# Tokens beside the last output tile, late products on TensorE, and row sums as columns, in a two-layer transformer kernel

## The reference

```python
for l in range(2):
    sh, sc, g = split(silu(c) @ w_mod[l] + b_mod[l])      # the same with c_ctx for the context tokens
    h = x * (1 + sc) + sh                                  # modulated tokens
    q, k, v, z = split(h @ w_in[l])
    y = neighbourhood_attention(q, k, v) if l == 0 else differential_attention(q, k, v)
    out = (y * silu(z)) @ w_out[l]
    x = layer_norm(ALPHA * x + (1 + g) * out)              # layer 0: the context tokens too
```

## Time and profile before

| | |
|---|---|
| median of 3 runs | 1866.39 us (1865.43 to 1867.48) |
| the profiled execution | 1866.36 us, its span 1864.3 us |
| TensorE busy | 1807.0 us, 97% of the span |
| VectorE busy | 1303.2 us, 70% |
| ScalarE busy | 928.0 us, 50% |
| GpSimd busy | 270.6 us, 15% |
| mean granted TensorE clock | 0.994 |

### The profile page before, as it was taken

How to read it: one execution, slowest core, us unless ns; L and a number is a source line. 1 busy time by engine, 2 the same in 40 slices (tenths; PEclk the granted TensorE clock), 3 DMA queues, 4 the chain that set the end, 5 groups by cost and what they waited for, 6 DMA issues and landing times. The chain is left out here.

```text
span 1864.3 us, 30823 instructions
## 1 busy us (share of the span) xinstructions
PE 1807.0 (97%) x10617; PEld 1557.2 (84%) x10617; DVE 1303.2 (70%) x2061; ACT 928.0 (50%) x1680; POOL 270.6 (15%) x219
## 2 busy tenths in 40 slices
PE   7999999999999999989989999999999999999997
PEld 3888888888988888868868988888888888898886
DVE  6677777777777868775867576674848484757658
ACT  2555555555555555550045545464737464554500
POOL 3100000000000000256331010101001010102951
PEclk9999999999999999989999999999999999999999
DMA  9512121213121212225411010101010000101343
GB/s 346 133 48 81 50 82 46 82 47 84 45 80 43 79 54 62 89 76 185 157 68 35 12 45 11 39 6 45 11 34 23 34 23 11 45 11 45 98 153 113
DMA packets 81967, 127.28 MB, mean 68 GB/s; under 512 B 49744, under 2 KB 49904, under 8 KB 81792
## 3 DMA queue, kind: packets, MB, share of 16 engines
q1 hardware_dynamic: 76048, 108.54, 18.8%
q0 software_dynamic: 2384, 8.39, 1.6%
q10 hardware_dynamic: 3488, 9.73, 1.3%
HBM read 108.90 MB, written 20.09 MB: 69 GB/s over the span
## 5 line engine op out<-in xcount | busy, mean ns | idle before, releaser
L536 PE MATMUL acc<-h_hi,w_hi 128*128 128x512 f32 (+1 forms) x1408 | 524.7, 373 | 2.4 <-DVE h_lo L461 1.3
L536 PE MATMUL acc<-h_hi,w_lo 128*128 128x512 f32 (+1 forms) x1408 | 509.1, 362 | 0.0
L536 PE MATMUL acc<-h_lo,w_hi 128*128 128x512 f32 (+1 forms) x1408 | 508.3, 361 | 0.0
L536 PEld LDWEIGHTS acc<-h_hi,w_lo 128*128 128x128 f32 x1408 | 265.5, 189 | 41.5
L536 PEld LDWEIGHTS acc<-h_hi,w_hi 128*128 128x128 f32 x1408 | 266.0, 189 | 38.7 <-DVE h_lo L461 3.7
L536 PEld LDWEIGHTS acc<-h_lo,w_hi 128*128 128x128 f32 x1408 | 266.4, 189 | 34.0
L1645 DVE TENSOR_REDUCE stats<-acc 128x1 f32<-128x1280 f32 x128 | 189.7, 1487 | 43.3 <-PE acc L1739 42.7
L1562 ACT ACTIVATE far_prob<-acc,stats 128x1280 f32<-128x1280 f32 x128 | 170.2, 1330 | 28.3 <-DVE stats L1645 26.5
L1569 ACT ACTIVATE far_pt<-acc 128x512 f32<-128x512 f32 (+1 forms) x192 | 101.1, 527 | 162.1 <-PE acc L1748 158.6
L1739 PE MATMUL acc<-k_dup,q_stack 128*128 128x512 f32 (+1 forms) x768 | 176.8, 367 | 1.8 <-ACT far_prob L1562 0.4
L1761 PE MATMUL acc<-far_pt,far_v 128*128 128x128 f32 x1280 | 172.7, 275 | 0.0
(11 more groups left out here) (192 smaller groups left out, 2920.5 us busy)
## 6 DMA issues: line engine op xcount, KB each, us to landing
w_raw<-in_w_in SPq DMA_DIRECT2D x64, 512.0 KB, 3.4
near_late_slots<-in_w_mod SPq DMA_DIRECT2D x64, 256.0 KB, 2.6
w_raw<-in_w_out SPq DMA_DIRECT2D x16, 512.0 KB, 3.3
w_raw<-y_t POOLq DMA_DIRECT2D x14, 448.0 KB, 5.2
y_t<-y SPq DMA_DIRECT2D x7, 640.0 KB, 3.0
modulation_rows<-in_w_scale SPq DMA_DIRECT2D x8, 512.0 KB, 6.9
modulation_rows<-in_w_mod SPq DMA_DIRECT2D x8, 512.0 KB, 6.7
out_rows<-in_x SPq DMA_DIRECT2D x8, 512.0 KB, 4.6
```

The lines of the kernel that those rows point to most:

```text
L536: mm = nc.tensor.matmul(m.bank(self.bank_of(j, c), w), wt[:, b % 2, k, :], ht[:, k, t0:t0 + w], start=(k == 0 and i == 0), stop=(k == KT - ...
```

## The change

It has three parts.

**Tokens beside the last output tile.** Tile 9's output product is cut into its eight k. After each, TensorE does `turn(0, k)`, and `mm_done` counts each k. `take_hi(0, k)` waits for the k-th piece alone, since that piece is the last reader of `h_hi[:, k]`. VectorE mixes tile 8's layer norm with `take_lo` of group 0, and tile 9's with that of group 1. ScalarE's `root` and `store` of these tiles move between its modulations, and so does the split of projection weights 1. For group 2, products follow turns at a distance of four.

**The last chunk.** Tile 5 is summed in step 3, and tiles 6 and 7 not on VectorE at all: `reduce_last` multiplies their 128x128 blocks with the two condition columns on TensorE and adds them to the accumulators' sums in PSUM. The load of tile 7 moves up between the loads of output weights 3 and 4. The output weights' high parts are taken one step earlier from the second on (two in step 2). The fillings move: two pieces in each of the steps 5, 7 and 9 in place of one in each of 4 to 9; the one at the end of step 9 stays.

**Row sums as columns.** In every chunk the accumulators' 128x128 blocks become the weights and a column of ones the moving operand, so the sums land as eight columns (4 blocks x 2 conditions) on 128 partitions. ScalarE copies 128x8, and SP stores them with two transfers of single 4-byte elements. The buffer is no longer shared with `factors`, so one wait of ScalarE goes (`repeat_factors`).

The diff, without the hunks for `ones` in place of `pick`, the name `cols` and the end count 32 in place of 16:

```diff
--- before.py
+++ after.py
...
@@ -167,8 +167,8 @@
         self.late_acc = sb("late_acc", [P, 2, 512])
-        self.shared = sb("row_or_factors", [P, 512])
-        self.late_row, self.factors = self.shared[0:2, :], self.shared[:, 0:2 * P]
+        self.shared = sb("cols_and_factors", [P, 2 * P + 8])
+        self.factors, self.late_cols = self.shared[:, 0:2 * P], self.shared[:, 2 * P:2 * P + 8]
...
@@ -399,22 +397,42 @@
+    def sums(self, bank, t, first, count):
+        return self.m.psum[:, bank, 2 * t + first:2 * t + first + count]
...
         pe.wait_ge(self.summed, CREDIT + c * 2 * KT + 2 * KT)
-        for cnd in range(2):
-            mm = self.nc.tensor.matmul(self.m.psum[0:2, bank, :], self.m.pick[:, cnd, :], self.acc[cnd],
-                                       start=(cnd == 0), stop=(cnd == 1))
+        for t in range(4):
+            for cnd in range(2):
+                mm = self.nc.tensor.matmul(self.sums(bank, t, cnd, 1), self.acc[cnd][:, t * P:(t + 1) * P], self.m.ones[:, :],
+                                           start=True, stop=True)
...
+    def reduce_last(self, pe, c, bank):
+        for u in (KT - 2, KT - 1):
+            pe.wait_ge(self.loaded[u % 2], CREDIT + c * 8 * KT + 16 * (u // 2 + 1))
+        pe.wait_ge(self.summed, CREDIT + c * 2 * KT + 2 * (KT - 2))
+        for t in range(4):
+            for u in (KT - 2, KT - 1):
+                self.nc.tensor.matmul(self.sums(bank, t, 0, 2), self.slots[u % 2][:, t * P:(t + 1) * P], self.m.cond_act[:, :, u],
+                                      start=(u == KT - 2), stop=False)
+            for cnd in range(2):
+                mm = self.nc.tensor.matmul(self.sums(bank, t, cnd, 1), self.acc[cnd][:, t * P:(t + 1) * P], self.m.ones[:, :],
+                                           start=False, stop=(cnd == 1))
+        mm.then_inc(self.reduced, 1)
     def take_row(self, act, c, bank):
-        act.wait_ge(self.row_stored, CREDIT + c * 16)
+        act.wait_ge(self.row_stored, CREDIT + c * 32)
         act.wait_ge(self.reduced, CREDIT + c * 1 + 1)
-        self.nc.scalar.activation(self.row, self.m.psum[0:2, bank, :], ACT.Copy, scale=0.5).then_inc(self.row_ready, 1)
+        self.nc.scalar.activation(self.cols, self.m.psum[:, bank, 0:8], ACT.Copy, scale=0.5).then_inc(self.row_ready, 1)
...
         sp.wait_ge(self.row_ready, CREDIT + c * 1 + 1)
-        sp.dma_start(self.mod_rows[:, bass.ds(c * 512 + ROW_PAD, 512)], self.row).then_inc(self.row_stored, 16)
+        for cnd in range(2):
+            dst = self.mod_rows[cnd, bass.ds(c * 512 + ROW_PAD, 512)].rearrange("(t p) -> p t", p=P)
+            sp.dma_start(dst, self.cols.rearrange("p (t c) -> p c t", c=2)[:, cnd, :], allow_slow_non_contiguous=True).then_inc(self.row_stored, 16)
@@ -1005,8 +1023,8 @@
     filled = {step: piece[0:2] for (step, half), piece in fill.items() if piece[3] == KT}
-    fill_last = {(4, MIDDLE): (0, 1), (5, MIDDLE): (1, 2), (6, MIDDLE): (2, 3), (7, MIDDLE): (3, 4), (8, MIDDLE): (4, 5),
-                 (9, MIDDLE): (5, 6), (9, END): (6, 7)}
+    fill_last = {(5, MIDDLE): (0, 2), (7, MIDDLE): (2, 4), (9, MIDDLE): (4, 6), (9, END): (6, 7)}
+    OUT_SPLITS = {2: (0, 1), 3: (2,), 4: (3,), 5: (4,), 6: (5,), 7: (6,), 8: (7,)}
@@ -1072,6 +1090,8 @@
                             out_w.load(sp, p, k)
+                            if k == 3:
+                                late.load(sp, c, 7)
@@ -1081,9 +1101,8 @@
                             load_bias(biases[1], c, kind)
-                    late.load(sp, c, 7)
                     if not last:
-                        for u in (KT, KT + 1):
+                        for u in (7, KT, KT + 1):
...
@@ -1178,8 +1197,6 @@
                         act.wait_ge(recip_done, CREDIT + c * COLS + (col + 1))
-                        if col == 0:
-                            act.wait_ge(late.row_stored, CREDIT + c * 16)
@@ -1211,8 +1228,9 @@
                             p.split_hi_part(act, c, 5)
-                        if 2 <= step < 2 + KT and last:
-                            out_w.split_hi(act, p, step - 2)
+                        if last:
+                            for k in OUT_SPLITS.get(step, ()):
+                                out_w.split_hi(act, p, k)
@@ -1299,7 +1317,9 @@
                             p.split_lo_part(v, nc.vector, c, 5)
-                        if NU - 3 <= step < NU:
+                        if step == 3 and last:
+                            late.sum(v, c, 5)
+                        if NU - 3 <= step < NU and not last:
@@ -1426,7 +1446,10 @@
                                 pe.wait_ge(p.evac, CREDIT + (c + 1) * p.evacs + 3)
-                            late.reduce(pe, c, 1 if last else 7)
+                            if last:
+                                late.reduce_last(pe, c, 1)
+                            else:
+                                late.reduce(pe, c, 7)
@@ -1502,9 +1525,10 @@
                 p.split_lo_part(pool, nc.gpsimd, 0, 0)
-                pool.wait_ge(before.mm_done, TOK_TILES)
...
                     for k in range(KT):
+                        if g == 0:
+                            pool.wait_ge(before.mm_done, TOK_TILES + k)
@@ -1537,15 +1561,19 @@
                 p.split_hi_part(act, 0, 0)
-                before.act_tile(act, TOK_TILES - 2)
...
                     tokens.modulate(act, 0, k)
-                before.root(act, TOK_TILES - 1)
-                act.wait_ge(before.mm_done, TOK_TILES)
-                p.split_hi_part(act, 0, 1)
+                    if k == 1:
+                        before.root(act, TOK_TILES - 2)
+                    if k == 5:
+                        before.store(act, TOK_TILES - 2)
...
                     tokens.modulate(act, 1, k)
+                    if k == 5:
+                        act.wait_ge(before.mm_done, before.done(TOK_TILES - 1))
+                        p.split_hi_part(act, 0, 1)
+                before.root(act, TOK_TILES - 1)
@@ -1617,24 +1645,31 @@
                 before.dve_start(v)
-                for i in range(TOK_TILES - 1):
+                for i in range(TOK_TILES - 2):
                     before.dve_tile(v, i)
-                v.wait_ge(before.mm_done, TOK_TILES)
+                last = TOK_TILES - 2
+                before.take_product(v, last)
+                before.add_residual(v, last)
...
                     tokens.take_lo(v, 0, k)
-                    if k == 1:
-                        before.take_product(v, TOK_TILES - 1)
-                    if k == 4:
-                        before.add_residual(v, TOK_TILES - 1)
-                before.moments(v, TOK_TILES - 1)
+                    if k == 0:
+                        before.moments(v, last)
+                    if k == 2:
+                        before.centre(v, last)
+                    if k == 3:
+                        before.normalise(v, last)
+                last = TOK_TILES - 1
+                before.take_product(v, last)
+                for k in range(KT):
+                    tokens.take_lo(v, 1, k)
+                    if k == 0:
+                        before.add_residual(v, last)
+                    if k == 3:
+                        before.moments(v, last)
...
                 p.split_lo_part(v, nc.vector, 0, 1)
-                for k in range(KT):
-                    tokens.take_lo(v, 1, k)
-                    if k == 1:
-                        before.centre(v, TOK_TILES - 1)
-                    if k == 3:
-                        before.normalise(v, TOK_TILES - 1)
+                before.centre(v, last)
+                before.normalise(v, last)
@@ -1703,15 +1738,19 @@
             def _(pe):
-                before.pe_part(pe)
-                pe.wait_ge(before.normed, 4)
-                pe.wait_ge(before.psum_free, TOK_TILES - 1)
-                for k in range(KT):
+                def turn_first(k):
+                    if k == 0:
+                        pe.wait_ge(before.normed, 4)
+                        pe.wait_ge(before.psum_free, TOK_TILES - 2)
                     tokens.turn(pe, 0, k)
+                before.pe_part(pe, turn_first)
...
                     pe.wait_ge(tokens.lo_done, k + 1)
+                    if k == 0:
+                        pe.wait_ge(before.psum_free, TOK_TILES - 1)
@@ -1719,11 +1758,12 @@
                 pe.wait_ge(before.normed, TOK_TILES)
-                for k in range(KT):
-                    tokens.turn(pe, 2, k)
-                for k in range(KT):
-                    pe.wait_ge(tokens.lo_done, 2 * KT + k + 1)
-                    p.product_part(pe, 0, 2, k, k + 1)
+                for n in range(KT + BEHIND):
+                    if n < KT:
+                        tokens.turn(pe, 2, n)
+                    if n >= BEHIND:
+                        pe.wait_ge(tokens.lo_done, 2 * KT + n - BEHIND + 1)
+                        p.product_part(pe, 0, 2, n - BEHIND, n - BEHIND + 1)
@@ -1976,7 +2016,7 @@
         gain, first = self.gain[i // LAT_TILES], self.bank_of(i, 0)
```

(22 more changed lines are left out.)

## The result

The changed kernel takes 1874.9 us (median of 6 runs, 1872.8 to 1879.5) against 1866.4 before (6 runs, 1865.4 to 1867.5). The ratio is 1.0047, with a 95% interval of 1.0036 to 1.0057. The forecast was 1852.3 us, with a range of 1848.5 to 1859.5. The profiled execution of after is the slowest of its six (1879.5 us, span 1877.7), so its losses are some 4 us above the median's.

A forecast was written before the change was run, and what follows sets the result against it. The prediction took TensorE, busy 97% of the span, as the bound, so gains come from filling its holes or shortening its list. 1866.4 - 8.2 - 5.5 - 0.4 = 1852.3 us, range 1848.5 to 1859.5.

The forecast's parts named there:

- The stores: Row-sum stores in every chunk: 1024 single-element pieces take 4.7 us over 16 engines, hidden, so counted as nothing.
- waits in ordinary chunks behind SP's stores: Sign that the forecast is wrong: TensorE waiting in ordinary chunks behind the row-sum stores; no size given.
- the rival with the stores: End of layer 0: element stores delay the barrier, 58.8 us late if on one engine, total 1911; chance 0.03.
- Part A: Tokens beside tile 9: interleaving turns with its product recovers TensorE's waits and half clock; gain 8.2 us, ends 6.4 and 9.9.
- The 1.7 us that I gave back: Tokens, before product (0,3): a new TensorE wait behind VectorE and the split of weights 1, taken off 9.9 us.
- The ring of three: Tokens: three buffers become the bound as GpSimd and VectorE slow each other; gain only 3 us, 1857.5; chance 0.12.
- group 2 gained nothing: Tokens, group 2: 6.7 us set by the ScalarE, GpSimd and VectorE chain, which interleaving doesn't shorten; gain counted as nothing.
- Part B: Last chunk of layer 0: removing VectorE's sums from steps 7 to 9 gains 5.5 us net, ends 3 and 7.
- where I had said about 15: Last chunk, sign of being right: steps 8 to 10 take about 15 us.
- where I had said under 1: Last chunk, sign of being right: TensorE's waits for `y` in step 9 fall under 1 us.
- where I had 3.4: Last chunk, `reduce_last`: sixteen small float32 products, 32 instructions, take 3.4 us in place of 1.8.
- Part C: Row sums as columns in seven chunks: 0.1 us less each, gain taken as 0.4 us, ends -1.0 and +0.8.

The follow-up runs named there:

- 1024 elements 64 bytes apart: Kernel with tokens' and last chunk's parts and row stores, plus 1024 extra 4-byte element stores per ordinary chunk, each 64 bytes from the next: 1853.0 us.
- the two extra places side by side: Kernel with tokens' and last chunk's parts and row stores, plus 1024 extra packed elements per ordinary chunk, the second 2 KB right behind the first: 1853.0 us.
- both parts and row stores: Changed kernel keeping the tokens' and last chunk's parts, but with the sums back as two rows stored in contiguous 2 KB pieces: 1853.2 us.
- the rows side by side: Changed kernel with its element stores, but a chunk's two rows adjacent in HBM instead of 16.9 KB apart, readers following: 1853.6 us.
- 16-byte pieces: Changed kernel with column sums stored as 128 pieces of 16 bytes per condition instead of 512 single elements: 1855.5 us.

## Why the prediction was wrong, step by step

**The stores were the step that failed.** I worked out 4.7 us for 1024 pieces from the queue's mean time of a packet and placed them under "the next use of those queues is tens of us away". Both halves were wrong. The mean was over other packets: the element writes have hardly any time of their own in the records (9 ns each), but packed sixteen to each 64 bytes, in two places far apart, they hold up what comes behind them, so `y`'s store lands in 20.1 us. And the next use is not tens of us away: it is 2.2 us away (`y`), 3.6 for the next weights, and the engines themselves turned out to depend on the block's end: ScalarE and VectorE stopped some 10 us behind the stores, TensorE 17. I had put it at nothing; the cost is 1874.9 - 1853.6 = 21.3 us. I had listed "waits in ordinary chunks behind SP's stores" as a sign of being wrong, but given it no price; the rival with the stores was put at the block's end, where only a little happened. There, after's wait in front of layer 1's first product is 1.45 us; with the tokens alone it is 0.33:

```profile
868.99 0.69 PE L2077 MATMUL acc<-h_hi,k_dup 128*128 128x512 f32 x2 [1.45 <-PEq L1072]
...
847.16 0.70 PE L2054 MATMUL acc<-h_hi,k_dup 128*128 128x512 f32 x2 [0.33 <-PEq L1054]
```

The Trainium skill, DMA: Bandwidth & Descriptors, Rules for kernel authors, warned of a last dimension that isn't contiguous. Its advice would have saved this kernel, but its reason, one descriptor for each element, isn't what cost the time here: 1024 elements 64 bytes apart cost nothing measurable.

**Part A was right in its size, with one loss in another place.** Forecast 8.2 us, measured 7.9. From the start of layer 1's block to the end of group 2, the trace of the kernel with the tokens alone has 966.62 - 847.16 = 119.5 us, before 975.85 - 848.25 = 127.6. Turns and products alternate, the clock stays at 1 (window, columns as above), and of the waits for modulated tokens 1.0 us is left:

```profile
925.00:967.00 42.00, 40.86 (x224) 32.77 (x223) 32.00 (x43) 18.51 (x31) 20.24 (x25) 1.00 0.21 76
...
PE acc L536 <- DVE h_lo L461: 0.8, 2, 0.5
PE acc L536 <- DVE w_lo L519: 0.2, 1, 0.2
```

The 1.7 us that I gave back came too, but elsewhere, so that the sum fits so closely is in part luck. From 938.02 to group 2 at 959.94 are 21.9 us, against 19.9 of work. The 2.0 lost are small holes within product (0,1), whose pieces follow `take_lo` at up to 1.1 us in place of 0.69:

```profile
951.42 0.50 PE L536 MATMUL acc<-h_hi,w_hi 128*128 128x512 f32 x1
952.23 0.40 PE L536 MATMUL acc<-h_hi,w_hi 128*128 128x512 f32 x1
953.23 0.50 PE L536 MATMUL acc<-h_hi,w_hi 128*128 128x512 f32 x1
954.36 0.50 PE L536 MATMUL acc<-h_hi,w_hi 128*128 128x512 f32 x1 [0.17 <-DVE w_lo L519]
```

The ring of three was not the bound, and group 2 gained nothing, as forecast.

**Part B was right.** Forecast 5.5 us. In after, the last chunk from its predecessor's row sums (754.36) to the products behind its steps (848.87) takes 94.5 us, before 830.66 - 730.59 = 100.1: a gain of 5.6. With row sums it is 95.3, a gain of 4.8, and 4.8 by the medians. That execution has the granted clock at 0.5 for 3.4 us from 792.8 on; the kernel with the two extra places side by side, with row sums too, has none there and takes 94.4. TensorE's waits from 730 to 850 with both parts and row stores, beside the earlier trace rows, show that 7.0 and 2.5 us became 3.5 and nothing. 1.5 us are new, 1.3 of them behind the sum of tile 5, and those for `near_pt_lo` in front of the factors' transposes grew from 2.3 to 3.5:

```profile
PE acc L1399 <- DVE y L1282: 3.5, 4, 1.6
PE acc L1384 <- DVE near_pt_lo L1274: 3.5, 4, 0.9
PE acc L1375 <- DVE near_pt_lo L1274: 1.5, 2, 1.3
```

From step 7's value products (810.92) to the products behind the steps (826.15) it takes 15.2 us there, where I had said about 15. The wait for `y` in step 9 is 1.2 us, where I had said under 1. `reduce_last` takes 847.97 - 844.48 = 3.5 us in after, where I had 3.4.

**Part C was right in its size and missed a clock.** With the rows side by side, five of the six distances are 95.35 to 95.38, so a chunk gains 0.1 us, as forecast. But the granted clock fell to 0.5 for 3.4 us behind the row sums at one place in eight there (161.6, distance 96.9), at two in eight with 16-byte pieces (638.0 and 825.7), and at two in after (660.7, which is part of the 20.4 us above, and 848.4); with sums as rows, at none. Each costs 1.7 us (half of 3.4). The window behind the last row sums with 16-byte pieces, and with row stores:

```profile
825.60:829.00 3.40, 3.40 (x13) 2.81 (x12) 1.71 (x4) 0.94 (x3) 3.16 (x7) 0.52 0.05 1
...
826.00:829.40 3.40, 3.40 (x18) 2.85 (x17) 1.70 (x4) 1.35 (x3) 3.16 (x7) 1.00 0.00 1
```

That eats the gain of C: 1853.6 with columns and 1853.2 with rows are equal within their spread. Whether the one-column products cause it was not tested by itself.

**The sum** 1866.4 - 8.2 - 5.5 - 0.4 = 1852.3 lies 1.3 us under the changed kernel with its rows side by side, and 22.6 under the changed kernel as it is.

## What to carry to other kernels

An element-wise store must be judged by where its elements land, not by their number: 4-byte writes packed sixteen to each 64 bytes of HBM, in two places far apart, held up the transfers of other queues too, and elements 64 bytes apart, or a store of whole rows, did not. When a transfer is called hidden, look at what else uses transfers in the next 20 us, and count the engines themselves among it: holding `y` for 12 us was free here and for 20 us was not. A releaser `remote`, where the product that is waited for ended long ago, meant a semaphore update that came late here, not a missing instruction. Give a price to each sign that would prove a forecast wrong; the sign without one was what happened.

## What the runs showed of the hardware

- Writes of 4 bytes: sixteen in each 64 bytes, in one place of 2 or 4 KB, hold `y`'s store until 10.9 to 12.6 us; eight in each 64 bytes, in two places, until 8.3; four pieces of 16 bytes, in two places, until 4.3; one in each 64 bytes leaves it at 3.1.
- Two places 16.9 KB or 256 KB apart, each packed, take 19.7 to 20.3 us, two places of twice the size 23.5. Why distance counts and size hardly does stays open.
- During such a block, the transfers of all queues seen crawl, instruction packets among them (two came 6 us late). TensorE's semaphore updates are in the trace up to 12.2 us behind the products that give them, and ScalarE and VectorE, which wait for them, stop from some 10 to 12 us behind the issue on. TensorE stops within products for 13.5 us in all, for a reason that no trace tells.
- The same stores at the same point of the program cost between 0.4 and 8.9 us in different chunks of one execution.
